# A residual kept in DRAM, attention heads in pairs, and two orders of work on VectorE and ScalarE

## The reference

```python
# first block
h = rms_norm(x, mix_norm_g)
c_b, c_c, c_u, f_q, f_k, f_v, f_g, s_q, s_k, s_v, gate_logits = split_proj(h @ w_in)
y_conv = short_conv_branch(c_b, c_c, c_u, conv_w)          # gated convolution over 3 tokens
y_fox = fox_branch(f_q, f_k, f_v, f_g, forget_bias)        # 8 heads of 64, causal, forget gates
y_swa = swa_sink_branch(s_q, s_k, s_v, rel_bias, sink)     # 8 heads of 64, 2 key heads, window 128
merged = sum(sigmoid(gate_logits[i]) * (y_i @ w_branch[i]) for i in range(3))
x = x + merged @ w_mix_out
...
# second block: HGRN2 mixer with key width 128, and a spatial gating branch
a_out = hgrn2_mixer(zq, zf_f, zf_b, zi, zg, lb_fwd, lb_bwd, hg_norm)
b_out = spatial_gating(zu, zv, sg_w, sg_b, sg_ln_g, sg_ln_b)
merged = sigmoid(ga) * (a_out @ w_a) + sigmoid(gb) * (b_out @ w_b)
x = x + rms_norm_2(merged @ w_out, norm_mix_post)
```

## Time and profile before

| | us |
|---|---|
| median of 3 runs | 1040.33 |
| lowest, highest | 1039.88, 1040.78 |
| the profiled execution | 1043.29 |
| its span (first to last instruction) | 1041.5 |

### The profile page before, as it was taken

The page is one execution under the profiler, slowest core; times in us unless marked ns, Lnnn a source line. Parts: engine busy times, 40 slices in busy tenths (PEclk is TensorE's granted clock), DMA queues, the critical chain, the costliest instruction groups (busy, mean ns, idle before and its releaser), DMA issues.

```text
span 1041.5 us, 17023 instructions
## 1 busy us (share of the span) xinstructions
PE 1030.0 (99%) x7276; PEld 918.4 (88%) x7276; DVE 745.7 (72%) x891; ACT 601.1 (58%) x728; POOL 6.6 (1%) x11
## 2 busy tenths in 40 slices
PE   9999999999999999999999999998999999999998
PEld 8999988899988988888889989997787888888887
DVE  5677865665654688776568899689947988776456
ACT  5565566436344464544447996698654765555443
POOL 2000000000000000000000000000000000000000
PEclk9999999999999999999999999999999999999999
DMA  9865445744634475655565556355544556554641
GB/s 306 215 193 189 160 146 163 236 162 150 215 122 162 156 231 189 193 177 176 182 202 163 162 163 190 94 164 162 163 162 143 171 189 215 189 188 150 228 156 41
DMA packets 141451, 182.74 MB, mean 175 GB/s; under 512 B 14132, under 2 KB 92064, under 8 KB 141376
## 3 DMA queue, kind: packets, MB, share of 16 engines
q1 hardware_dynamic: 141160, 181.45, 54.7%
q10 hardware_dynamic: 216, 0.21, 0.1%
HBM read 180.40 MB, written 1.25 MB: 174 GB/s over the span
## 4 chain that ended last, share of the span: by engine, by line
PE 91%; ACT 4%; DVE 3%; issue 2%; DMA 0%; SPq 0%; DVEq 0%; ACTq 0%
PE ps L552 22%; PE ps L585 22%; PE ps L641 21%; PE ps L587 11%; PE ps L694 2%; PE ps L1189 2%; PE ps L582 1%; ACT whi L1247 1%; PE ps L696 1%; PE ps L1050 1%; DVE wlo L1881 1%; PE ps L832 1%; PE ps L929 1%; PE ps L951 1%; PE ps L658 1%
## 5 line engine op out<-in xcount | busy, mean ns | idle before, releaser
L1881 DVE TENSOR_TENSOR wlo<-raw,whi 128x2048 fp32r<-128x2048 f32 (+3 forms) x170 | 378.1, 2228 | 147.8 <-ACT whi L1247 147.3
L1247 ACT ACTIVATE whi<-raw 128x2048 fp32r<-128x2048 f32 (+1 forms) x167 | 310.6, 1864 | 87.5 <-PE ps L552 28.8
L585 PE MATMUL ps<-ha,whi 128*128 128x512 f32 x640 | 224.1, 396 | 0.0
L552 PE MATMUL ps<-ha,whi 128*128 128x256 f32 x1008 | 185.0, 286 | 0.0
L587 PE MATMUL ps<-ha,wlo 128*128 128x256 f32 x640 | 178.2, 278 | 0.0
L552 PEld LDWEIGHTS ps<-ha,whi 128*128 128x128 f32 x1008 | 157.7, 192 | 1.8 <-DVE wlo L1881 1.0
L585 PEld LDWEIGHTS ps<-ha,whi 128*128 128x128 f32 x640 | 120.2, 188 | 28.5
L641 PE MATMUL ps<-whi,ha 128*128 128x512 f32 x448 | 143.1, 401 | 2.1 <-DVE wlo L1881 2.1
L552 PE MATMUL ps<-ha,wlo 128*128 128x256 f32 x504 | 142.6, 283 | 0.0
L587 PEld LDWEIGHTS ps<-ha,wlo 128*128 128x128 f32 x640 | 120.5, 188 | 0.1
L585 PE MATMUL ps<-pr,whi 128*128 128x512 f32 x330 | 116.5, 397 | 0.0
(11 more groups left out here) (407 smaller groups left out, 1649.8 us busy)
## 6 DMA issues: line engine op xcount, KB each, us to landing
raw<-in_w_in SPq DMA_DIRECT2D x54, 1024.0 KB, 5.3
raw<-in_w_ffn_gate SPq DMA_DIRECT2D x11, 1024.0 KB, 5.1
raw<-in_w_ffn_up SPq DMA_DIRECT2D x11, 1024.0 KB, 5.1
raw<-in_w_gate SPq DMA_DIRECT2D x11, 1024.0 KB, 5.1
raw<-in_w_up SPq DMA_DIRECT2D x11, 1024.0 KB, 5.1
raw<-in_w_xkv SPq DMA_DIRECT2D x8, 1024.0 KB, 5.0
raw<-in_w_ffn_down SPq DMA_DIRECT2D x8, 1024.0 KB, 4.7
raw<-in_w_down SPq DMA_DIRECT2D x8, 1024.0 KB, 4.7
```

The lines of the kernel that those rows point to most:

```text
L552: mm = e.matmul(ps[0:width, m * T:(m + 1) * T], a[:, kk, m * width:(m + 1) * width], b[:, off + k, :], start=k == 0 and j == 0 and m % 2 = ...
L585: e.matmul(banks[s][:, at_:at_ + 512], wh[:, kk, c], H[2][:, :, k, :], start=k == 0, stop=False, skip_group_check=True)
L1247: e.activation(h, r, ACT.Copy).then_inc(*hi_done.up(n))
L1881: e.tensor_tensor(l, r, h.bitcast(F32), ALU.subtract).then_inc(*lo_done.up(n))
```

## The change

Five edits:

1. **Residual kept.** ACT copies x, feature-major, from banks 1 and 2 into `X` right after the first turn, and writes it from there to a DRAM tensor `x_columns`. After the convolution's halves are made, SP reads it back into `X`. The second load, turn and copy of x go. TensorE waits for the two copies before it writes banks 1 and 2 again; ACT waits for the write before it uses the memory of `X` for another tile.
2. **Paired heads.** Steps with even t do two heads at once, on all engines; odd steps do none. Sliding-window scores are contracted over the 64 rows of their own key head, and the two heads of a pair are on different rows. Six transposes go into bank 3, values' half too, and ACT copies 768 columns at once. GpSimd's zero fill of the queries goes.
3. **Weight halves first in the second mixer.** In part i = 1, `hi` and `lo` come before `mix_exps` at every level, and not at the first alone.
4. **The turn inside a unit** (`between`) comes at its last k of four, not at the second.
5. **`ml_lo` of the first half** comes before the second half's first sums.

```diff
...
-    PT = [at(f"pt{i}", [P, 384], F32, kb) for i, kb in enumerate((140.5, 142, 203, 204.5))]
+    PT2 = [at(f"pt{i}", [P, 768], F32, kb) for i, kb in enumerate((140.5, 203))]
+    PT = [PT2[i // 2][:, 384 * (i % 2):384 * (i % 2) + 384] for i in range(4)]
...
+    x_kept = nc.dram_tensor("x_columns", [P, 8 * T], F32).ap().rearrange("p (k t) -> p k t", k=8)
...
-        e.wait_ge(*pe_val.on(("attn", 3)))
-        e.wait_ge(*v_split.on(("y", 3)))
-        e.dma_start(x_tm2[:, :, :], x_v).then_inc(s_x2, 16)
+        e.wait_ge(*v_split.on("conv"))
+        e.dma_start(X[:, :, :], x_kept).then_inc(s_x2, 16)
...
-                if between is not None and (t, kk) == (1, 1):
+                if between is not None and (t, kk) == (1, 3):
...
+        e.wait_ge(*a_evac.on(("x", 0)))
         unit_in_two("fk", HA, 1, v_split.on(("x", 1)))
...
+        e.wait_ge(*a_evac.on(("x", 1)))
         unit_tm("fv", 0, HA, 2, v_split.on(("x", 3)))
...
-        def scores(i):
-            kind, h = heads[i]
-            S = Sb[i % 2]
-            if kind == "fox":
-                qq, kk_ = fq[h % 2][:, h // 2, :], fk[h % 2][:, h // 2, :]
-            else:
-                qq, kk_ = sq_[h // 4][:, h % 4, :], sk[:, :]
-            if i == 0:
+        def scores(p):
+            if p == 0:
                 e.wait_ge(*p_pad.on("heads"))
                 e.wait_ge(*v_evac.on("fk"))
                 e.wait_ge(*a_evac.on(("fv", 1)))
-                e.wait_ge(*v_stat.on("first sums"))
-            if i == 1:
                 e.wait_ge(*v_stat.on("key sums"))
                 e.wait_ge(*a_stat.on("query sums"))
-            if i == 8:
-                e.wait_ge(*p_pad.on(("local query", 1)))
+            if p == 4:
                 e.wait_ge(*v_evac.on("sq"))
                 e.wait_ge(*v_evac.on("sk"))
-            if i >= 2:
-                e.wait_ge(*v_soft.on(("max", i - 2)))
-            e.matmul(S[:, 0:P], qq[:, 0:P], kk_[:, 0:P], start=True, stop=True, skip_group_check=True)
-            e.matmul(S[:, P:P + T], qq[:, P:T], kk_[:, 0:T], start=False, stop=True,
-                     skip_group_check=True).then_inc(*pe_score.up(("attn", i)))
-
-        def probs(i):
-            L = Lb[i % 3]
-            e.wait_ge(*v_soft.on(("p", i)))
-            if i == 0:
+            if p >= 1:
+                e.wait_ge(*v_soft.on(("max", 2 * p - 1)))
+            sides = []
+            for i in (2 * p, 2 * p + 1):
+                kind, h = heads[i]
+                if kind == "fox":
+                    sides.append((fq[h % 2][:, h // 2, :], fk[h % 2][:, h // 2, :]))
+                else:
+                    r = OWN[h // 4]
+                    sides.append((sq_[h // 4][r, h % 4, :], sk[r, :]))
+            for c, q_, n in ((0, slice(0, P), P), (P, slice(P, T), T)):
+                for u in range(2):
+                    qq, kk_ = sides[u]
+                    mm = e.matmul(Sb[u][:, c:c + n], qq[:, q_], kk_[:, 0:n], start=c == 0, stop=True,
+                                  skip_group_check=True)
+                    if c:
+                        mm.then_inc(*pe_score.up(("attn", 2 * p + u)))
+
+        def probs(p):
+            if p == 0:
                 e.wait_ge(*v_stat.on(("rows", "mem")))
-            if i >= 1:
-                e.wait_ge(*a_soft.on(("pt", i - 1)))
-            for j in range(3):
-                mm = e.transpose(Tb[:, j * P:(j + 1) * P], L[:, j * P:(j + 1) * P], ident[:, :])
-            mm.then_inc(*pe_turn.up(("attn", i)))
+            if p >= 1:
+                e.wait_ge(*a_soft.on(("pt", 2 * p - 1)))
+            if p >= 2 and p % 2 == 0:
+                e.wait_ge(*v_split.on(("y", p // 2 - 1)))
+            for i in (2 * p, 2 * p + 1):
+                e.wait_ge(*v_soft.on(("p", i)))
+                for j in range(3):
+                    c = (3 * (i % 2) + j) * P
+                    mm = e.transpose(banks[3][:, c:c + P], Lb[i % 3][:, j * P:(j + 1) * P], ident[:, :])
+                mm.then_inc(*pe_turn.up(("attn", i)))
 
         def values(j):
             e.wait_ge(*a_soft.on(("pt", 4 * j + 3)))
@@ -861,12 +869,12 @@
             mm.then_inc(*pe_val.up(("attn", j)))
 
         def attention(t):
-            if t >= 4 and t % 4 == 3:
-                values(t // 4 - 1)
-            if 3 <= t < 19:
-                probs(t - 3)
-            if 1 <= t < 17:
-                scores(t - 1)
+            if t in VALUES_AT:
+                values(VALUES_AT.index(t))
+            if t % 2 == 0 and 4 <= t <= 18:
+                probs(t // 2 - 2)
+            if t % 2 == 0 and 2 <= t <= 16:
+                scores(t // 2 - 1)
...
-        e.wait_ge(s_x2, 16)
-        turn("x2", x_tm2, 3, 0, a_soft.on(("pt", 15)))
-        turn("x2", x_tm2, 2, 1, v_evac.on("br00"))
         unit_tm("br10", 0, Y, 0, v_evac.on("br01"), K=4)
         e.wait_ge(*v_stat.on(("merged", 0)))
         turn("mg", mg, 1, 0, v_evac.on("br02"))
-        unit_tm("br11", 0, Y, 3, a_evac.on(("x2", 0)), K=4, off=4)
-        unit_tm("br12", 0, Y, 2, a_evac.on(("x2", 1)), K=4, off=8)
+        unit_tm("br11", 0, Y, 3, a_soft.on(("pt", 15)), K=4, off=4)
+        unit_tm("br12", 0, Y, 2, v_evac.on("br00"), K=4, off=8)
...
+    VALUES_AT = (7, 11, 15, 19)
...
         hi(3)
+        for g in range(2):
+            e.wait_ge(*v_split.on(("x", 2 * g + 1)))
+            e.activation(X[:, 4 * g:4 * g + 4, :], banks[1 + g][:, :], ACT.Copy).then_inc(*a_evac.up(("x", g)))
...
         hi_for("fk")
+        e.wait_ge(*a_evac.on(("x", 1)))
+        e.dma_start(x_kept, X[:, :, :]).then_inc(s_kept, 16)
...
+        e.wait_ge(s_kept, 16)
...
-        def probs(i):
-            e.wait_ge(*pe_turn.on(("attn", i)))
-            if i >= 4:
-                e.wait_ge(*pe_val.on(("attn", i // 4 - 1)))
-            e.activation(PT[i % 4][:, :], Tb[:, 0:384], ACT.Copy).then_inc(*a_soft.up(("pt", i)))
+        def probs(p):
+            e.wait_ge(*pe_turn.on(("attn", 2 * p + 1)))
+            if p >= 2:
+                e.wait_ge(*pe_val.on(("attn", p // 2 - 1)))
+            e.activation(PT2[p % 2][:, :], banks[3][:, 0:768], ACT.Copy).then_inc(*a_soft.up(("pt", 2 * p + 1)))
...
-            if 3 <= t < 19:
-                probs(t - 3)
-            if 1 <= t < 17:
+            if t in VALUES_AT:
+                y_hi(VALUES_AT.index(t))
+            if t % 2 == 0 and 4 <= t <= 18:
+                probs(t // 2 - 2)
+            if t % 2 == 0 and 2 <= t <= 16:
+                softmax(t - 2)
                 softmax(t - 1)
...
-            if g == 0:
-                for j in range(2):
-                    e.wait_ge(*pe_turn.on(("x2", j, 1)))
-                    e.activation(X[:, 4 * j:4 * j + 4, :], banks[(3, 2)[j]][:, :], ACT.Copy).then_inc(*a_evac.up(("x2", j)))
...
-            if (i, t) == (1, 1):
+            if i == 1:
                 hi(u + 2)
                 mix_exps(i, t)
             else:
...
-        def softmax(i, meanwhile=None):
+        def row_max(i):
...
-            if meanwhile is not None:
-                meanwhile()
+
+        def normalize(i):
+            L, mx = Lb[i % 3], sc[:, 64 + 8 * (i % 3):72 + 8 * (i % 3)]
             e.wait_ge(*a_soft.on(("exp", i)))
-            if not w:
+            if heads[i][0] != "fox":
...
         def attention(t, meanwhile=None):
-            if 1 <= t < 17:
-                softmax(t - 1, meanwhile)
-            if t >= 7 and t % 4 == 3:
-                y_lo(t // 4 - 1)
+            pair = (t - 2, t - 1) if t % 2 == 0 and 2 <= t <= 16 else ()
+            for i in pair:
+                row_max(i)
+            if meanwhile is not None:
+                meanwhile()
+            for i in pair:
+                normalize(i)
+            if t in VALUES_AT:
+                y_lo(VALUES_AT.index(t))
...
-        e.wait_ge(*a_evac.on(("x2", 1)))
+        e.wait_ge(s_x2, 16)
...
-        merged2(1, 0)
         ml_lo(0, 0)
         ml_lo(0, 1)
+        merged2(1, 0)
         merged2(1, 1)
...
-        for u in range(2):
-            e.wait_ge(*p_pad.on("heads" if u == 0 else ("local query", 0)))
-            e.memset(sq_[u][OTHER[u], :, :], 0.0).then_inc(*p_pad.up(("local query", u)))
```

More of the change, by code:

```diff
@@ L152, in build @@
     MG = (at("mg_hi", [P, 8, T], F32R, 128), at("mg_lo", [P, 8, T], F32R, 136))
-    x_tm2 = at("x_tm2", [P, 2, 1024], F32, 196)
     nsq = at("nsq", [P, 8, T], F32, 164)
@@ L255, in build @@
         "gain0", "gain", "relb", "m3", "sink", "fbias", "masks"))
-    s_small, s_scr, s_bias, s_x2 = (sem(f"ld_{n}") for n in ("small", "rows", "bias", "x_again"))
+    s_small, s_scr, s_bias, s_x2, s_kept = (sem(f"ld_{n}") for n in ("small", "rows", "bias", "x_again", "x_kept"))
     s_ws, s_bsb, s_lng, s_lnb, s_p, s_out = (sem(f"ld_{n}") for n in ("ws", "bsb", "lng", "lnb", "p", "out"))
@@ L878, in tensor @@
         unit("sq", 1, HA, 0)
-        attention(1)
         linear("cc", HA, 1, None, a_evac.on("sv"), lambda i: attention(2 + i))
@@ L893, in tensor @@
         e.wait_ge(*v_split.on("conv"))
```

(14 more changed lines are left out.)

## The result

The changed kernel takes 1035.65 us (median of four executions, three of them 1034.86 to 1035.68) beside 1040.55 us for the kernel before on the same chip: ratio 0.9947, 95% interval 0.9928 to 0.9967. The fourth execution took 1249.6 us at a mean granted clock of 0.753, and the ratio leaves it out. On a second chip it was 1035.28 (median of five) beside 1040.46 us, ratio 0.9951 (0.9938 to 0.9965). That is 4.9 to 5.2 us of the 6.95 forecast. The profiled execution is one of 1034.86 us with a span of 1033.0.

What follows compares the result with a forecast made beforehand. TensorE, busy 1030.0 of 1041.5 us, was taken as the bound. Gains of 1.75 + 2.2 + 0.3 + 1.6 + 1.1 = 6.95 us off the 1040.33 us median gave 1033.4 us, range 1031.2 to 1037.3.

Steps and rivals of the forecast that it cites:

- Residual: Branch products: sixteen transposes of x leave TensorE between two products, 1.75 us gained.
- Early copies, DRAM write and read: Near the start: two ACT copies, a 1 MB write and its read back cost 0; upper end 1 us for the write.
- Pairs: First mixer's attention: four pairs of sliding-window heads, scores on two row halves side by side, gain 2.2 us.
- the ratio 0.55 from the values product: Attention: values product takes 1.45 us against 2.64 at the scores' rate; applied to scores, a pair costs 0.73 for 1.32.
- First head's wait: Attention: the first head's scores come one unit later and no longer wait for DVE, 0.3 us gained.
- Softmax of a pair: Attention: a pair's softmax takes some 5 us on DVE and ACT, ready within two units of 11 us; cost 0.
- Rival (d): Attention: a pair holds ACT and DVE so long that the low half is late; 26 us lost, 1060, chance 0.03.
- Halves first: Second mixer: 3.8 us of wait and slow unit go, new wait of 1.6 and 0.5 at last scores; 1.6 gained.
- Rival (b): Second mixer: the new 1.6 us wait before the first `ga` unit lowers the clock; price 1.7 us, 1035.1, chance 0.14.
- Merged features: Turns of the merged features and product behind: later turn and earlier low half gain 1.1 us, ends 0.7 and 1.3.
- Rival (c): Second mixer: the wait for bank 0 is shorter than forecast and all 3.8 us stay gained; 1031.3, chance 0.05.
- Sum: Whole kernel: 1.75 + 2.2 + 0.3 + 1.6 + 1.1 = 6.95 us gained, 1033.4 us forecast.

Runs made afterwards that it cites:

- the two experiments on rows: Changed kernel with sliding-window scores over all 128 rows again (1036.27 us); changed kernel with both matmuls of one row half before those of the other (1038.03 us).

## Why the prediction was right or wrong

The direction and the range held, and each mechanism is there. The forecast of 1033.4 was 2.25 us too low, for two reasons: one term was mis-sized, and one saving exists in about half the executions only. Point by point, forecast and measured:

- **Residual**: 1.75 forecast, 1.77 measured, alone and in the whole change. Early copies, DRAM write and read: 0, and 0 measured.
- **Pairs**: 2.2 forecast, 1.0 measured (0.98 from the comparison with full rows). The direction was right, the step that failed is the ratio 0.55 from the values product. I let that row stand for a group of matmuls half as long, and took it that the row carried the cost of changing shape. It carries only one side of it. The changed kernel has a unit behind the second values product, and it takes 5.67 us (132.87), not 5.48: 0.2 us lie outside the row. The trace of the kernel before shows the same cost in the three transposes behind a values product, 0.48 us against 0.33 elsewhere (start us, us, engine, line; the second row stands behind the product at 104.34 in the earlier trace rows):

```profile
97.87 0.33 PE ps L843 x3
...
105.79 0.48 PE ps L843 x3
```

  An estimate from the two lengths, which takes column halves and row halves as alike (no run tests that): 1536 columns in 1.45 us and 768 in 0.86 make 0.59 us for 768 and 0.27 us that don't depend on the length. So a pair takes 0.59 + 0.27 + 0.2 = 1.06 us for 1.31. The prediction asked whether halves run side by side, which they do, and gave too little to what surrounds them. It set against each other two sections of the Trainium skill: "TensorE: Matmul & The Clock Gate", Part 3 (matmuls on different row groups overlap), and "TensorEngine Tiling (Array Packing)", Key Properties (a change of mode drains the engine). The runs fit both: the scores gain 0.45 us a pair, and the unit behind takes back 0.21. That a drain is what costs the 0.21 us is the page's account; no run here isolates it.
- **First head's wait**: 0.3 forecast. The stretch gives 1.45 to 1.49 in all, so with 0.98 for the halves about 0.5 is left. The wait (0.27 us by the time line) and the first head's scores, which took 0.89 us behind it for 0.65 elsewhere, make 0.5; some 0.1 us is lost again, since a unit behind a values product loses 0.2 where the transposes lost 0.15.
- **Softmax of a pair**: forecast in time, and no wait of TensorE in that stretch. Rival (d) falls.
- **Halves first**: 1.6 forecast, 1.47 measured against an execution with the low clock. Its parts came as written: `gb` 1.0 us earlier from DVE, a new wait of 1.7 us (1.6 forecast) at bank 0, 0.4 us (0.5) at the last scores. What the prediction didn't see is that the slow unit behind the 2.1 us wait is an event of some executions: 21 of 39. In the others the edit is worth 0.39 us. The step was "wait and slow unit are 2.1 + 1.7 = 3.8 us", taken from one profile as a property of the kernel. The profiled execution had the low clock; by the count, one with it and one without are about equally likely.
- **Rival (b)**, the new wait takes the clock down: of the executions with this wait of 1.6 to 1.7 us, 8 of the changed kernel, 11 with the halves alone and one each of the two experiments on rows, none reads 0.998. So it left the clock alone 21 times. A wait of 2.5 us there took it down once in four, and one of 1.9 us did at the last scores, in a single execution. By the Trainium skill ("TensorE: Matmul & The Clock Gate", Part 1) the low clock is the default, which activity releases; the traces agree in so far as each of their four falls stands behind a wait of 1.9 us or more. In these runs the same wait in the same program decides now one way, now the other. What makes the difference from one execution to the next stays open.
- **Merged features**: 1.1 forecast, 1.07 alone. In the whole change it is 0.97 against the kernel before and 1.03 against the one with the weight halves first, which has the same short wait ahead of its last scores.
- **Rival (c)** has a slip of 0.1 in its sum: with all 3.8 us kept, the forecast would be 1033.4 - 2.2 = 1031.2, not 1031.3. Nothing hangs on it.
- **Sum**: the stretches give 1.77 + 1.45 + 1.47 + 1.03 = 5.7 us against an execution with the low clock, and 1.77 + 1.45 + 0.39 + 1.03 = 4.6 against one without. The spans with a short feed-forward give 1038.8 - 1033.4 = 5.4 and 1037.8 - 1033.4 = 4.4. The medians lie between, at 4.9 and 5.2. Of the 2.05 us missing from 6.95, 1.2 are the pairs. About 0.5 is the clock, by an estimate: 1.08 us in 18 of 39 executions.

## What to carry to other kernels

Where an engine gains by packing two small products side by side, price them together with the work behind them, against the same products unpacked: here 0.21 us of a gain of 0.45 went to the unit behind. A wait of the bounding engine can cost more than its length, here 2.1 us of wait and 1.7 in the unit behind, but count over several executions how often the clock falls before the slow unit goes into a sum. When a wait is removed by reordering an engine that is busy all through the stage, it comes back at that engine's next delivery; look for work that stands ahead of that delivery and that it doesn't need, as the last low half here, and move this work behind it.

## What the runs showed of the hardware

**Pairs of matmuls have two speeds at one granted clock.** The measured part of the first block's feed-forward takes 148.15 to 148.16 us in five traces (the kernel before twice, the changed kernel, two of its variants) and 145.68 to 145.69 in the other eight. No wait makes the difference; the pairs of matmuls are longer. In the time line of TensorE, first the kernel before, then the changed one (start us, us, line, operation):

```profile
450.15 0.40 PE L585 MATMUL ps<-ha,whi 128*128 128x512 f32 x1
450.38 0.28 PE L587 MATMUL ps<-ha,wlo 128*128 128x256 f32 x1
450.50 0.40 PE L585 MATMUL ps<-ha,whi 128*128 128x512 f32 x1
...
451.21 0.40 PE L585 MATMUL ps<-ha,whi 128*128 128x512 f32 x1
```

```profile
450.02 0.40 PE L585 MATMUL ps<-ha,whi 128*128 128x512 f32 x1
450.25 0.28 PE L587 MATMUL ps<-ha,wlo 128*128 128x256 f32 x1
450.37 0.39 PE L585 MATMUL ps<-ha,whi 128*128 128x512 f32 x1
...
451.07 0.39 PE L585 MATMUL ps<-ha,whi 128*128 128x512 f32 x1
```

Three pairs take 1.06 us (450.15 to 451.21) in the one and 1.05 (450.02 to 451.07) in the other; from 410 us to the end of the stage the mean is 0.353 and 0.347 us a pair. Both speeds occur in every trace, within one execution. The short form starts at the slow pace too (0.355 us a pair from 399.5 to 406 us in the kernel with the weight halves first) and changes to 0.347 behind one pair of 0.37 us that stands 6.5 us after the turn of the spatial weights; the long form has that pair too, and keeps its pace. The second block's feed-forward does the same, later: in the kernel before 0.354 from 810 to 835 us and 0.347 from 845 on. The run times show it: of 39 spans of the kernel before, 25 lie between 1037.4 and 1039.0 us and 14 between 1040.5 and 1041.6; the 14 are 3 of 21, 7 of 11 and 4 of 7 on the three chips. That is a step as large as half of this change, so two single profiles can't be subtracted: 2.5 of their 8.5 us are this. What brings the change of pace stays open.

**The two halves of the rows work side by side whatever the order of issue.** Two fp32 score matmuls on one half of the rows (128 and 256 columns) followed by two on the other take the same 0.86 us as the four in turn, and 1.31 us over all rows.
